# Inverse roots of queries and keys spread from the upper 64 rows of the array, directly behind the state value row's product in the lower 64

## Chip, cores and metric

The kernel runs on one core of one Trainium2 chip. The metric is the device time of one execution in microseconds (us); the median of three runs is given. TensorE multiplies and writes to the eight PSUM banks, VectorE and ScalarE move and change data, GpSimd (POOL) works on SBUF alone, SyncE (SP) issues DMAs.

## What is computed

One inference step of a decoder layer, for 256 prompt tokens and 8 sample tokens (one new token in each of 8 sequences), so 264 columns in all. A half feed-forward block, then a mixer with two branches that share one input projection, then a second half feed-forward block. The parts that matter here:

```python
qa, ka, va, qr, kr, vr, gr, ga, gb = split(h @ w_in)
# branch A: attention, 3 groups x 8 heads x 64, queries and keys normed per head
qa = rope(rmsnorm(qa, a_q_norm)) * A_SCALE
ka = rope(rmsnorm(ka, a_k_norm))
# branch B: retention, 4 heads, q and k of 256, v of 512; for each of the 8 sequences
state = state * gamma[h] + outer(k, v)      # 256 x 512, read, changed and written back
o = q @ state
```

The root mean square of queries and keys is over 64 features of a head. The retention state is 8 sequences x 4 heads, 32 matrices of 256 x 512.

## The kernel before

The activations stand transposed: features on the partitions, 264 tokens in the free dimension. A weight is streamed from HBM in halves of 128 x 1024 (512 KB). ScalarE rounds each half to fp32r (`wh`), VectorE takes the rest (`wl`, L428), and TensorE makes three passes for each 128 x 128 tile: `wh` with the high part of the activations, `wh` with their low part, `wl` with the high part (`three_passes`, L448 to L450). A half that makes one output tile is eight steps (k = 0 to 7) of three passes, `pe_wide_half`. Other small work of TensorE is put between the steps through the list `between`.

The order of work is written out by hand, half by half. After the projections of retention q, k and v come 16 halves of the gate (`gr`), then 24 halves for queries and keys (`qk`), 12 for the values (`v`), 8 for gate B (`gb`), 16 for projection B (`pb`), and so on. From the first query half on, the halves are numbered as slots: slots 0 to 11 are queries, 12 to 23 keys, 24 to 35 values. `slot_steps` says what TensorE does between the steps of slot s, and `qk_slot` what VectorE does in it.

State update. For each of the 32 states (sequence b, head h) TensorE broadcasts the value row of the sample to all partitions: `pe_state_v` multiplies a selector column, `pick`, repeated 128 times, with `vr_hl`, which has the high part of the eight value rows in partitions 0 to 7 and the low part in partitions 32 to 39, zeros elsewhere. The result is 128 x 512 in bank 6. VectorE then adds it, times k, to the state (`dve_state`, L1078), and TensorE multiplies the state with q in four narrow column groups (`pe_state_o`, L1087). States 0 to 7 are done in the gate's halves, at step 0 (for the first head once at step 5), states 8 to 31 in slots 1 to 32 (`STATE_SLOT`), each at step 0; at step 6 of every second slot stand the products with q and the sums of squares (`pe_qk_ms`, L927). Each state value product waits until VectorE has done the update before.

Norm of queries and keys. When the 12 query tiles have been squared and summed, ScalarE takes the root, VectorE its inverse, and ScalarE puts the 24 rows of 256 inverse roots (two heads in each of 12 tiles) in `qk_rinv`; `qk_rhl` has their high part in partitions 0 to 31 and their low part in 32 to 63 (`act_qk_rhi`, `dve_qk_rlo`). `pe_qk_spread` multiplies them with `sel` (128 x 128 for each tile), so that each row of a tile gets the inverse root of its head: two products of 256 columns for a pair of tiles, u, in the two halves of bank 4. VectorE multiplies the pair of tiles with it (`dve_qk_norm`, L1010). The next spread waits for that norm (`qk_done`). `SPREAD_AT` gives the slot of each spread: 18 to 23 for the queries, 28 to 33 for the keys, at step 4. In each slot VectorE's order is: shuffle for the rotation, the norm of this slot's spread, copy of a value tile, the update for the next slot's state value product, low part of the weights for four halves ahead.

After the last norm, `sp.wait_ge(qk_done, AT)` (L1545) lets SP load the first keys of the caches (L1236), with which VectorE starts in the first half of `gb` (`dve_key_product`, L1292). Ahead of this wait SP has issued the store of the last state and two large copies of the caches (`roll_more`, L1485).

A product that works on 64 partitions only is there once in the kernel before: `pe_scores` (L1146) multiplies queries and keys of 64 features, for two heads at a time, one on the lower and one on the upper 64 rows. Transposes and the products a_dec by v_ret (L829) work on fp32 as it is, all others named here on fp32r.

Of the kernel before, what the change touches and what calls it, by code (L numbers as in the profile page):

```python
# [7 lines left out]
F32 = mybir.dt.float32  # L8
F32R = mybir.dt.float32r
ALU = mybir.AluOpType  # L10
ACT = mybir.ActivationFunctionType
AX = mybir.AxisListType

P = 128
D = 1024
KD = D // P
S = 256
# [7 lines left out]
AH, AE = 8, 64  # L25
AW = AH * AE
AT = G * AW // P
RH, RQ, RV = 4, 256, 512
# [68 lines left out]
def build_tables():  # L97

    tab = np.zeros((P, NTAB), np.float32)

    def put(name, value):
        a, b = TABLES[name]
        value = np.asarray(value, np.float32)
        tab[:value.shape[0], a:b] = value.reshape(value.shape[0], b - a)

    pos = np.concatenate([np.arange(S), np.full(B, PAST)]).astype(np.float32)
    half = AE // 8
    inv = (np.float32(500000.0) ** (-np.arange(half, dtype=np.float32) / np.float32(half))).astype(np.float32)
    ang = (pos[None, :] * inv[:, None]).astype(np.float32).astype(np.float64)
    cos_a, sin_a = np.ones((P, T)), np.zeros((P, T))  # L110
    for base in (0, AE):
        for r in range(2):
            cos_a[base + r * half:base + (r + 1) * half] = np.cos(ang)
            sin_a[base + r * half:base + (r + 1) * half] = (-1.0 if r == 0 else 1.0) * np.sin(ang)
    put("cos_a", cos_a)
    put("sin_a", sin_a)
    head = np.zeros((P, HEADW))
    head[:AE, 2 * (AT - 1)] = 1.0
    head[AE:, 2 * (AT - 1) + 1] = 1.0
    put("head", head)  # L120
    put("sel", np.concatenate([np.eye(32), np.eye(32), np.zeros((64, 32))])[:, 0:2 * AT])
    put("seq", np.broadcast_to(np.eye(B).reshape(1, B * B), (P, B * B)))
    inv_r = (np.float32(1.0) / np.float32(10000.0) ** np.linspace(0.0, 1.0, P, dtype=np.float32)).astype(np.float32)
    ang_r = (pos[None, :] * inv_r[:, None]).astype(np.float32).astype(np.float64)
    put("cos_r", np.cos(ang_r))
    put("sin_r", np.sin(ang_r))
    token = 2 * (np.arange(S) % P) + np.arange(S) // P

    def allowed(g, queries, keys):
        dil = GROUPS[g][1]  # L130
        dist = token[queries][:, None] - token[keys][None, :]
        return np.where((dist >= 0) & (dist % dil == 0) & (dist // dil <= P), 0.0, NEG)

    first, second, both = slice(0, P), slice(P, S), slice(0, S)
    put("mask", np.concatenate([allowed(0, first, both), allowed(1, first, first), allowed(2, first, first),
                                allowed(0, second, both)], axis=1))
    gamma = 1.0 - 2.0 ** (-5.0 - np.arange(RH))
    decay = np.zeros((P, RH, 2, P))
    j, i = np.arange(P)[:, None], np.arange(P)[None, :]
    for h in range(RH):  # L140
        decay[:, h, 0] = np.where(i >= j, gamma[h] ** np.maximum(i - j, 0), 0.0)
        decay[:, h, 1] = gamma[h] ** (P + i - j)
    put("decay", decay)
    put("ident", np.eye(P))
    put("ones", np.ones((P, P)))
    put("blocks", np.kron(np.eye(2), np.ones((AE, AE))))
    kdec = np.zeros((P, RH, 2))
    for h in range(RH):
        for c in range(2):
            kdec[:, h, c] = gamma[h] ** (S - 1 - c * P - np.arange(P))  # L150
    put("kdec", kdec)
    put("gamma", np.broadcast_to(gamma, (P, RH)))
    row = np.arange(P)
    seq_at, head_at = row // 32, np.where(row % 32 < G * AH, row % 32, -1)
    put("rsel", (32 * (head_at // AH) + 28 + seq_at)[:, None] * np.where(head_at < 0, 0, 1)[:, None] == np.arange(100)[None, :])
    put("own_pick", (head_at[:, None] >= 0) & (head_at[:, None] % AH == np.arange(32)[None, :] // 4)
        & (seq_at[:, None] == np.arange(32)[None, :] % 4))
    put("own_head", np.arange(AH)[None, :] == (row % 32)[:, None])
    put("own_seq", np.arange(B)[None, :] % 4 == row[:, None] // 32)
    put("pick", (np.arange(PICK)[:, None] % 32 == np.arange(B)[None, :]))  # L160
    put("eps", np.full((P, 1), EPS))
    return tab


def trunk_step(nc, xT, tables, gains, w16, w11, cache0, cache1, cache2, state_in,
# [3 lines left out]
    with ExitStack() as ctx:  # L169
# [27 lines left out]
        pick = fixed("pick", [B], F32R)  # L197
# [54 lines left out]
        qk_rinv = at("qk_rinv", 93504, [S])  # L252
        qk_rinv4 = at("qk_rinv4", 90368, [AE])
        qk_rhl = at("qk_rhl", 94528, [S], F32R)
# [4 lines left out]
        vr_hl = at("vr_hl", 16384, [RH * RV], F32R)  # L259
# [37 lines left out]
        sel = nc.alloc_sbuf_tensor_at("sel", [P, AT * P], F32R, offset=tab_at + 4 * TABLES["cos_r"][0])  # L297
# [7 lines left out]
        bank4, bank5, bank6, bank7 = aux45[:, 0], aux45[:, 1], aux67[:, 0], aux67[:, 1]  # L305

        def sem(name):
# [27 lines left out]
        cleared, pick_done = sem("cleared"), sem("pick_done")  # L335
        qk_sq_done, qk_sq_s, qk_ms_psum, qk_rms_done, qk_rinv_done = (
            sem("qk_sq_done"), sem("qk_sq_s"), sem("qk_ms_psum"), sem("qk_rms_done"), sem("qk_rinv_done"))
        qk_rows, qk_rhi, qk_rlo, qks_ms, qks_rms, qks_rinv, qks_done = (
            sem("qk_rows"), sem("qk_rhi"), sem("qk_rlo"), sem("qks_ms"), sem("qks_rms"), sem("qks_rinv"), sem("qks_done"))
# [4 lines left out]
        vr_hi, vr_lo, vb_psum, state_scaled, state_new = (  # L344
            sem("vr_hi"), sem("vr_lo"), sem("vb_psum"), sem("state_scaled"), sem("state_new"))
# [29 lines left out]
        for q in range(QUADS):  # L375
            for s in range(2):
                n = 2 * q + s
# [564 lines left out]
        def act_qk_rhi(act, which):  # L942
            act.wait_ge(qk_rinv_done, which + 1)
            if which:
                act.wait_ge(qk_spread, AT // 2 * which)
            for e in range(4):
                nc.scalar.activation(qk_rinv[0:32, e * AE:(e + 1) * AE], qk_rinv4[32 * e:32 * e + 32], ACT.Copy).then_inc(qk_rows, 1)
            act.wait_ge(qk_rows, 4 * which + 4)
            nc.scalar.activation(qk_rhl[0:32], qk_rinv[0:32], ACT.Copy).then_inc(qk_rhi, 1)

        def dve_qk_rlo(dve, which):
            dve.wait_ge(qk_rhi, which + 1)
            nc.vector.tensor_tensor(qk_rhl[32:64], qk_rinv[0:32], qk_rhl[0:32].bitcast(F32),
                                    ALU.subtract).then_inc(qk_rlo, 1)

        def pe_qk_samples(pe):
# [39 lines left out]
        def pe_qk_spread(pe, u):  # L996

            pe.wait_ge(qk_rlo, 2 * u // AT + 1)
            if u:
                pe.wait_ge(qk_done, u)  # L1000
            for n in range(2):
                i = (2 * u + n) % AT
                last = nc.tensor.matmul(bank4[:, n * S:(n + 1) * S], sel[:, i * P:(i + 1) * P], qk_rhl[:], start=True, stop=True)
            last.then_inc(qk_spread, 1)

        def dve_qk_norm(dve, u):
# [33 lines left out]
        def pe_state_v(pe, s):  # L1040

            b, h = divmod(s, RH)
            if s:
                pe.wait_ge(state_new, 2 * s)
            else:
                pe.wait_ge(pick_done, 1)
                pe.wait_ge(vr_lo, 1)
                pe.wait_ge(q_owned, 1)
            if s == 2:
                pe.wait_ge(vr_lo, 2)  # L1050
            nc.tensor.matmul(bank6[:, :], pick[:, b:b + 1].to_broadcast([P, P]), vr_hl[:, h * RV:(h + 1) * RV], start=True, stop=True).then_inc(vb_psum, 1)  # L1051

        def act_rows_hi(act, part):

# [370 lines left out]

        fi1, fo1, p_qr, p_kr, p_vr, p_gr, p_qk, p_v, p_gb, p_pb, p_ga, p_pa, p_wo, fi2, fo2 = phases

        SPREAD_AT = {18 + u: u for u in range(AT // 2)}
        SPREAD_AT.update({28 + u: AT // 2 + u for u in range(AT // 2)})
        PAIR_STEP = 6  # L1430
        STATE_TURN = {s: [slot for slot in (s - 2, s - 1) if slot in STATE_SLOT] for s in range(2, 3 * AT - 3, 2)}
        STATE_TURN[3 * AT - 3] = [3 * AT - 4]
# [562 lines left out]
        def _(pool):  # L1995
# [20 lines left out]
            pool.wait_ge(os_psum, 6)  # L2016
            for n in (4, 5):
                pool.wait_ge(state_stored[n], 32)
            nc.gpsimd.memset(qk_rhl[:].bitcast(F32), 0.0).then_inc(cleared, 1)
            for t in range(2 * AT):  # L2020
                pool_qk_rot(pool, p_qk, t)
            pool_pack(pool)
# [17 lines left out]
        def _(pe):  # L2040
# [38 lines left out]
            def slot_steps(s):  # L2079


                steps = {k: [] for k in range(KD)}
                if s in STATE_SLOT:
                    steps[0].append(lambda: pe_state_v(pe, STATE_SLOT[s]))
                if s == 2:
                    steps[PAIR_STEP].append(lambda: pe_state_o(pe, EARLY_STATES - 1))
                for slot in STATE_TURN.get(s, ()):
                    steps[PAIR_STEP].append(lambda slot=slot: pe_state_o(pe, STATE_SLOT[slot]))
                if s % 2 == 0 and 2 <= s <= 2 * AT:
                    steps[PAIR_STEP] += [lambda: pe_qk_ms(pe, s - 2), lambda: pe_qk_ms(pe, s - 1)]  # L2090
                if s == 2 * AT + 2:
                    steps[1].append(lambda: pe_qk_samples(pe))
                if s in SPREAD_AT:
                    steps[4].append(lambda: pe_qk_spread(pe, SPREAD_AT[s]))
                return steps

            def bank_waits():
# [26 lines left out]
            for t in range(AT):  # L2124
                steps = slot_steps(RH * p_qk.quads + t)
# [170 lines left out]
```

## Time and profile before

| | us |
|---|---|
| median of 3 runs (lowest, highest) | 890.43 (890.13, 890.57) |
| profiled execution | 890.51 |
| its span | 888.4 |
| TensorE busy (PE) | 882.4, 99% |
| weight loads (PEld) | 854.5, 96% |
| VectorE busy (DVE) | 623.7, 70% |
| ScalarE busy (ACT) | 484.6, 55% |
| GpSimd busy (POOL) | 218.5, 25% |
| share of the time for which DMA packets were under way | 9 tenths or more in most of the 40 slices |

The profile was taken in one execution. A row of the timeline has the start in us from the span's start, the duration, the engine, the line of the kernel, the operation, what it writes and reads, and its shape; "128*64" before a matmul's shape is rows by columns of the array. Instructions of the same line that follow each other are merged, with their count behind x. PE is a matmul, PEld the weight load that belongs to it. A matmul's duration is a latency; the next one usually starts long before it ends. Idle time before an instruction stands in brackets, with what ended it.

### The profile page before, as it was taken

The numbers are of one execution on the slowest core, as the hardware profiler recorded it, in microseconds if no ns is written. First come the engines' busy times: TensorE is split into PE (matmuls) and PEld (weight loads), VectorE is DVE, ScalarE is ACT, GpSimd is POOL, SyncE is SP. The second block draws the span as 40 slices with busy tenths as digits, with TensorE's granted clock in tenths as the row PEclk, the third lists the DMA queues.
The fourth block names the chain that finished last, engine by engine and source line by source line (L and its number), as shares of the span: only waits on it lengthen the run. The fifth ranks groups of instructions, "written<-read, shape, count | busy, mean of one in ns | idle before, by whom it ended". The sixth has DMA issues, their size and how long they took to land.

```text
span 888.4 us, 19101 instructions
## 1 busy us (share of the span) xinstructions
PE 882.4 (99%) x7772; PEld 854.5 (96%) x7772; DVE 623.7 (70%) x917; ACT 484.6 (55%) x746; POOL 218.5 (25%) x239
## 2 busy tenths in 40 slices
PE   9999999999999999999999999999999999999998
PEld 8999999999999999999999999889899999999998
DVE  6666665568985588888887769985458666665543
ACT  6443444455544677677776556566646544443342
POOL 0433331004740000029875006000000043333000
PEclk9999999999999999999999999999999999999999
DMA  9998878999888778999997899787889899989771
GB/s 349 384 344 301 303 258 299 371 345 414 294 313 303 287 284 312 340 376 358 417 387 260 319 362 350 284 291 284 306 324 329 274 371 396 368 290 347 224 195 44
DMA packets 62054, 281.20 MB, mean 317 GB/s; under 512 B 7792, under 2 KB 8944, under 8 KB 60240
## 3 DMA queue, kind: packets, MB, share of 16 engines
q10 hardware_dynamic: 39024, 131.61, 43.6%
q1 hardware_dynamic: 22944, 148.37, 43.5%
q8 instruction: 62, 1.02, 0.5%
q14 instruction: 24, 0.20, 0.1%
HBM read 256.70 MB, written 111.32 MB: 414 GB/s over the span
## 4 chain that ended last, share of the span: by engine, by line
PE 90%; DVE 5%; DMA 2%; ACT 1%; issue 1%; ACTq 0%; POOL 0%; DVEq 0%
PE acc L448 16%; PE acc L449 15%; PE acc L450 15%; PE att L448 11%; PE att L449 10%; PE att L450 10%; DMA raw<-w 2%; PE aux L1087 2%; DVE wl L428 2%; PE att L1146 1%; PE att L1181 1%; PE att L1198 1%; PE aux L1051 1%; PE att L829 1%; PE att L746 1%
## 5 line engine op out<-in xcount | busy, mean ns | idle before, releaser
L428 DVE TENSOR_TENSOR wl<-raw,wh 128x1024 fp32r<-128x1024 f32 (+2 forms) x278 | 333.5, 1201 | 182.6 <-ACT wh L422 178.0
L422 ACT ACTIVATE wh<-raw 128x1024 fp32r<-128x1024 f32 (+2 forms) x278 | 275.2, 994 | 169.9 <-PE acc L450 89.6
L448 PE MATMUL acc<-hh,wh 128*128 128x264 f32 x496 | 145.4, 293 | 0.1
L449 PE MATMUL acc<-hl,wh 128*128 128x264 f32 x496 | 140.7, 284 | 0.0
L450 PE MATMUL acc<-hh,wl 128*128 128x264 f32 x496 | 140.6, 283 | 0.0
L448 PE MATMUL acc<-xh,wh 128*128 128x264 f32 x416 | 119.0, 286 | 0.4 <-DVE xl L556 0.4
L448 PE MATMUL att<-xh,wh 128*128 128x264 f32 x416 | 118.6, 285 | 0.4 <-DVE xl L556 0.3
L449 PE MATMUL att<-xl,wh 128*128 128x264 f32 x416 | 117.9, 283 | 0.0
L449 PE MATMUL acc<-xl,wh 128*128 128x264 f32 x416 | 117.8, 283 | 0.0
L450 PE MATMUL acc<-xh,wl 128*128 128x264 f32 x416 | 117.8, 283 | 0.0
L450 PE MATMUL att<-xh,wl 128*128 128x264 f32 x416 | 117.8, 283 | 0.0
L448 PEld LDWEIGHTS acc<-hh,wh 128*128 128x128 f32 x496 | 93.4, 188 | 2.3 <-issue 0.9
L449 PEld LDWEIGHTS acc<-hl,wh 128*128 128x128 f32 x496 | 93.5, 188 | 1.3
L450 PEld LDWEIGHTS acc<-hh,wl 128*128 128x128 f32 x496 | 93.2, 188 | 0.0
L448 PEld LDWEIGHTS acc<-xh,wh 128*128 128x128 f32 x416 | 78.3, 188 | 1.5 <-DVE xl L556 0.8
L630 POOL CAST uh<-product 128x264 fp32r<-128x264 f32 x44 | 31.0, 705 | 198.0 <-DVE product L619 198.0
L448 PEld LDWEIGHTS att<-xh,wh 128*128 128x128 f32 x416 | 78.3, 188 | 0.9 <-DVE xl L556 0.5
L449 PEld LDWEIGHTS att<-xl,wh 128*128 128x128 f32 x416 | 78.4, 188 | 0.1
L449 PEld LDWEIGHTS acc<-xl,wh 128*128 128x128 f32 x416 | 78.4, 188 | 0.0
L450 PEld LDWEIGHTS att<-xh,wl 128*128 128x128 f32 x416 | 78.0, 187 | 0.0
L450 PEld LDWEIGHTS acc<-xh,wl 128*128 128x128 f32 x416 | 78.0, 187 | 0.0
L598 ACT ACTIVATE silu<-square 128x264 f32<-128x264 f32 x44 | 18.7, 425 | 100.1 <-DVE square L612 100.1
(276 smaller groups left out, 2067.9 us busy)
## 6 DMA issues: line engine op xcount, KB each, us to landing
raw<-w ACTq DMA_DIRECT2D x207, 512.0 KB, 7.0
state<-state_in SPq DMA_DIRECT2D x32, 512.0 KB, 9.7
state_out<-state SPq DMA_DIRECT2D x32, 512.0 KB, 6.9
raw<-w ACTq DMA_DIRECT2D x32, 384.0 KB, 5.6
kv<-cache SPq DMA_DIRECT2D x24, 512.0 KB, 6.1
raw<-w ACTq DMA_DIRECT2D x32, 320.0 KB, 5.3
raw<-w SPq DMA_DIRECT2D x9, 512.0 KB, 9.5
kv_out<-cache SPq DMA_DIRECT2D x3, 960.0 KB, 7.2
```

The lines of the kernel that those rows point to most:

```text
L422: nc.scalar.activation(wh[n % HI_RING][:, 0:slot_size(n)], raw[n % RAW_RING][:, 0:slot_size(n)], ACT.Copy).then_inc(hi_done, 1)
L428: nc.vector.tensor_tensor(wl[n % RAW_RING][:, 0:slot_size(n)], raw[n % RAW_RING][:, 0:slot_size(n)], wh[n % HI_RING][:, 0:slot_size(n)].bi ...
L448: nc.tensor.matmul(out, w_hi, xh, start=first, stop=False)
L449: nc.tensor.matmul(out, w_hi, xl, start=False, stop=False)
L450: return nc.tensor.matmul(out, w_lo, xh, start=False, stop=last)
L598: nc.scalar.activation(silu[:, j // 2], gated[:, j // 2], ACT.Silu).then_inc(silu_done, 1)
L630: nc.gpsimd.tensor_copy(u_h, product[:, s]).then_inc(u_hi, 1)
L746: nc.tensor.transpose(rows[:, c * P:(c + 1) * P], part, ident)
L829: nc.tensor.matmul(out, v_ret[:, 0, cols], a_dec[:, 0:S], start=True, stop=False)
L1051: nc.tensor.matmul(bank6[:, :], pick[:, b:b + 1].to_broadcast([P, P]), vr_hl[:, h * RV:(h + 1) * RV], start=True, stop=True).then_inc(vb_p ...
L1087: last = nc.tensor.matmul(bank7[32 * e:32 * e + B, h * P:(h + 1) * P], q_own[:, 2 * h + p, b], state_of(s)[:, p * RV + e * P:p * RV + (e + ...
L1146: last = nc.tensor.matmul(out, qk[rows, t, qb:S:2], keys[:, qb] if n else keys, start=True, stop=True)
```

## The change

The spread's operands move to partitions 64 to 127: `sel` has its two unit blocks there, `qk_rinv` and `qk_rhl` are written at partitions 64 to 95 and 96 to 127. Both products are cut to 64 partitions: the state value product takes partitions 0 to 63 of `pick` and `vr_hl`, the spread partitions 64 to 127 of `sel` and `qk_rhl`. The spread goes from step 4 to step 0, right behind the slot's state value product where there is one. `SPREAD_AT` is set anew: 18, 19, 21, 22, 23, 25 for the queries and 29 to 34 for the keys; all but 31, 33 and 34 are slots with a state value product. The memset that cleared `qk_rhl` on GpSimd is gone, as no partition outside the cleared half is read.

```diff
-    put("sel", np.concatenate([np.eye(32), np.eye(32), np.zeros((64, 32))])[:, 0:2 * AT])
+    put("sel", np.concatenate([np.zeros((64, 32)), np.eye(32), np.eye(32)])[:, 0:2 * AT])
...
-                nc.scalar.activation(qk_rinv[0:32, e * AE:(e + 1) * AE], qk_rinv4[32 * e:32 * e + 32], ACT.Copy).then_inc(qk_rows, 1)
+                nc.scalar.activation(qk_rinv[64:96, e * AE:(e + 1) * AE], qk_rinv4[32 * e:32 * e + 32], ACT.Copy).then_inc(qk_rows, 1)
             act.wait_ge(qk_rows, 4 * which + 4)
-            nc.scalar.activation(qk_rhl[0:32], qk_rinv[0:32], ACT.Copy).then_inc(qk_rhi, 1)
+            nc.scalar.activation(qk_rhl[64:96], qk_rinv[64:96], ACT.Copy).then_inc(qk_rhi, 1)
...
-            nc.vector.tensor_tensor(qk_rhl[32:64], qk_rinv[0:32], qk_rhl[0:32].bitcast(F32),
+            nc.vector.tensor_tensor(qk_rhl[96:P], qk_rinv[64:96], qk_rhl[64:96].bitcast(F32),
                                     ALU.subtract).then_inc(qk_rlo, 1)
...
-                last = nc.tensor.matmul(bank4[:, n * S:(n + 1) * S], sel[:, i * P:(i + 1) * P], qk_rhl[:], start=True, stop=True)
+                last = nc.tensor.matmul(bank4[:, n * S:(n + 1) * S], sel[64:P, i * P:(i + 1) * P], qk_rhl[64:P], start=True,
+                                        stop=True)
...
-            nc.tensor.matmul(bank6[:, :], pick[:, b:b + 1].to_broadcast([P, P]), vr_hl[:, h * RV:(h + 1) * RV], start=True, stop=True).then_inc(vb_psum, 1)
+            nc.tensor.matmul(bank6[:, :], pick[0:64, b:b + 1].to_broadcast([64, P]), vr_hl[0:64, h * RV:(h + 1) * RV],
+                             start=True, stop=True).then_inc(vb_psum, 1)
...
-        SPREAD_AT = {18 + u: u for u in range(AT // 2)}
-        SPREAD_AT.update({28 + u: AT // 2 + u for u in range(AT // 2)})
+        SPREAD_AT = {18: 0, 19: 1, 21: 2, 22: 3, 23: 4, 25: 5, 29: 6, 30: 7, 31: 8, 32: 9, 33: 10, 34: 11}
...
-            nc.gpsimd.memset(qk_rhl[:].bitcast(F32), 0.0).then_inc(cleared, 1)
...
                 if s in STATE_SLOT:
                     steps[0].append(lambda: pe_state_v(pe, STATE_SLOT[s]))
+                if s in SPREAD_AT:
+                    steps[0].append(lambda: pe_qk_spread(pe, SPREAD_AT[s]))
...
-                if s in SPREAD_AT:
-                    steps[4].append(lambda: pe_qk_spread(pe, SPREAD_AT[s]))
```

## Rows read from the trace of the kernel before

**Rows 1.** Windows: stretch, busy us of each engine, clock, DMA share, GB/s.
```profile
240.00:515.00 275.00, 274.78 (x2661) 261.30 (x2660) 215.27 (x291) 179.99 (x282) 89.90 (x115) 1.00 0.90 329
537.00:564.00 27.00, 27.00 (x227) 26.68 (x226) 26.72 (x44) 15.79 (x21) 11.52 (x7) 1.00 0.99 375
```
**Rows 2.** Timeline of TensorE around one state value product.
```profile
435.38 0.28 PE L450 MATMUL att<-hh,wl 128*128 128x264 f32 x1
...
435.38 0.19 PEld L1051 LDWEIGHTS aux<-vr_hl,pick 128*128 128x128 f32 x1
...
435.50 0.39 PE L1051 MATMUL aux<-vr_hl,pick 128*128 128x512 f32 x1
...
435.73 0.28 PE L448 MATMUL acc<-hh,wh 128*128 128x264 f32 x1
```
**Rows 3.** Timeline of TensorE around one pair of spread products.
```profile
451.88 0.40 PE L1003 MATMUL att<-qk_rhl,sel 128*128 128x256 f32 x2
452.12 0.28 PE L448 MATMUL acc<-hh,wh 128*128 128x264 f32 x1
```
**Rows 4.** Timeline of TensorE around the first attention scores, in narrow windows.
```profile
562.34 0.28 PE L450 MATMUL acc<-obh,wl 128*128 128x264 f32 x1
562.55 0.51 PE L1146 MATMUL att<-qk 64*128 64x256 f32 x2
...
563.35 0.40 PE L1146 MATMUL att<-qk 64*128 64x128 f32 x4
...
563.46 0.28 PE L1146 MATMUL att<-qk 64*128 64x128 f32 x2
563.67 0.39 PE L448 MATMUL acc<-obh,wh 128*128 128x264 f32 x1
563.90 0.28 PE L449 MATMUL acc<-obl,wh 128*128 128x264 f32 x1
```
**Rows 5.** Groups of matmuls by shape: busy us, mean ns, idle before.
```profile
L829 PE MATMUL att<-a_dec,v_ret 128*128 128x256 f32 x32 | 9.6, 380 | 0.0
L1146 PE MATMUL att<-qk 64*128 64x256 f32 x32 | 5.8, 441 | 0.0
```
**Rows 6.** Timeline of the weight loads before the first scores.
```profile
562.54 0.20 PEld L1146 LDWEIGHTS att<-qk 64*128 64x128 f32 x2
```
**Rows 7.** Timeline of TensorE behind a group of narrow products.
```profile
438.78 0.39 PE L448 MATMUL acc<-hh,wh 128*128 128x264 f32 x1
439.01 0.29 PE L449 MATMUL acc<-hl,wh 128*128 128x264 f32 x1
```
**Rows 8.** Timeline of slots 21 and 22: state value products, update, norm.
```profile
462.50 0.39 PE L1051 MATMUL aux<-vr_hl,pick 128*128 128x512 f32 x1
...
463.00 1.41 DVE L1078 SCALAR_TENSOR_TENSOR state<-aux,kr_s,state 128x512 f32<-128x512 f32 x2 [1.52 <-PE aux L1051]
...
465.81 0.67 DVE L1010 TENSOR_TENSOR qk<-qk,att 128x512 f32<-128x512 f32 x1
...
465.87 0.39 PE L1051 MATMUL aux<-vr_hl,pick 128*128 128x512 f32 x1
```
**Rows 9.** Timeline at the change from slot 18 to slot 19.
```profile
454.10 0.66 DVE L1010 TENSOR_TENSOR qk<-qk,att 128x512 f32<-128x512 f32 x1
...
454.56 0.39 PE L1051 MATMUL aux<-vr_hl,pick 128*128 128x512 f32 x1
```
**Rows 10.** The cache copies before the keys: durations of issue, first and last start, landing.
```profile
L1485 SPq DMA_DIRECT2D kv_out<-cache x2: 665/790/915, 507.3 to 508.0; - x2
...
DMA to landing us min/median/max: 8.2/9.3/10.4
```
**Rows 11.** Timeline of SP's key loads and of VectorE until it uses them.
```profile
512.66 1.50 SPq L1236 DMA_DIRECT2D kv<-cache  x3
...
516.20 0.42 DVE L732 COPY v_tok<-att 128x256 f32<-128x256 f32 x1
...
525.48 1.22 DVE L1292 TENSOR_TENSOR kv<-kv,att 128x1024 f32<-128x1024 f32 x1 [0.56 <-DMA kv<-cache]
```

## The prediction

> **What bounds the kernel now.** I read the windows view first. Over the stretch of the retention gate and the attention projections, 240 to 515 us, TensorE is busy 274.78 of 275.00 us at a granted clock of 1.00, VectorE 215.27 us [rows 1]. But busy time is a sum of overlapping latencies here: a 128x264 pass is drawn with 0.28 us, while the next matmul starts 0.12 us after it [rows 2]. So the cost of a matmul is the distance from its start to the next start, and that is what I read everywhere below. As TensorE has no idle time to speak of, what is added between two starts is added to the end, and what is taken out is gained, unless another engine's work then comes late.
>
> The state value product (one per sequence and head, 32 in all) costs 0.23 us: it starts at 435.50 and the next pass at 435.73. Its weight load started at 435.38, under the pass ahead of it, so nothing is exposed [rows 2]. A pair of spread products costs 0.24 us (451.88 to 452.12) [rows 3]. Twelve such pairs are 2.9 us, which is the most that the change could hide.
>
> **What the change removes.** Nine of the twelve spreads (slots 18, 19, 21, 22, 23, 25, 29, 30, 32) now stand directly behind a state value product; slots 31, 33 and 34 have no state. The two products work on different halves of the array and write different banks. That such products run side by side is seen in the attention scores, which already work on 64 rows: two of 256 columns are both finished 0.51 us after the first one started [rows 4], where a single one takes 0.50 us (twice the mean of 441 ns less 380, see below) [rows 5]. So a pair that has the state product beside it costs about nothing: 9 x 0.24 = 2.15 us gained. The removed memset on POOL and the renamed partitions of the small copies cost or give nothing: POOL's memset has nobody waiting for its count, and the copies have the same number of columns.
>
> **What it adds: two changes of the array's shape around every state product.** This is the term that decides. Until now the state product contracts over all 128 partitions, as the passes on either side do. Afterwards it contracts over 64, and so do the spreads. The scores show what going to 64 rows and back costs [rows 4 to 6]:
> - going in, the first score starts 0.21 us after the last full pass (562.34 to 562.55), not 0.12: +0.09. Its weight load begins only at 562.54, beside it and not under the pass ahead [rows 6].
> - so the first product waits for its own weights: of the 32 score products of 256 columns, half are the first of a group. Their mean is 441 ns, where the same shape on full rows takes 380 [rows 5]. If the others take 380 too, the first ones take 502, so +0.12.
> - coming back, the last scores start at 563.46, the first full pass at 563.67: 0.21 us, where the products before had 0.11 (563.35 to 563.46): +0.10.
> - the first full pass has its load exposed: 563.67 to 563.90 is 0.23, not 0.12: +0.11 [rows 4].
>
> That is 0.42 us for one trip by rounded rows; I take 0.41. The narrow products on 8 and 32 columns pay the same way back: behind them a full pass is drawn with 0.39 us and the next starts 0.23 after it [rows 7]. So it isn't a peculiarity of the scores.
>
> There are 32 state products, none of which stands next to a group that changes the shape already: the narrow groups are at step 6 of a half, the state product at step 0 (in the first head at step 5). The three lone spreads make one trip each. 35 x 0.41 = +14.35 us. No state product of the gate phase gets anything in return, since no spread runs there, and 24 minus 9 in the slots get nothing either. Bounds: without the exposed load on the way in (the state product's load is 128 wide as the scores' was, so I don't expect that) a trip is 0.30 and the sum 10.5; the whole scores group, 1.56 us from 562.34 to 563.90, less two passes of 0.12, four pairs of 128 columns at 0.11 and two of 256 at twice that, leaves 0.44 for its trip [rows 4], and 35 x 0.45 is 15.75.
>
> The Trainium skill, "TensorEngine Tiling (Array Packing)", section "Key Properties", states that changing the tiling mode, and not just the tile, drains TensorE. That is a rule against this change, and the late loads and starts of the scores agree [rows 4, 6]. The same skill, "TensorE: Matmul & The Clock Gate", section "Measured speedup vs the span model", counts about 4 ns for each further tile of a pack; by that rule alone, with no drain, the sum would be the gain of 2.15 us and no more.
>
> **What it adds: a norm that must be finished earlier.** A spread waits until VectorE has consumed the one before from bank 4 (the norm, L1010). Behind the state product it stands four steps, twelve passes of 0.12 or 1.4 us, earlier in its slot than at step 4, and the main passes of TensorE stand behind it. The tight place is slot 22. VectorE's order in slot 21 is state update, low part of the weights, shuffle, norm: the state product of slot 21 starts at 462.50, the update at 463.00, the norm ends at 465.81 + 0.67 = 466.48, which is 3.98 us after the slot's start; slot 22 starts at 465.87, after 3.37 us [rows 8]. With the trip and without the spread at step 4 the slot becomes 3.37 + 0.41 - 0.24 = 3.54 us. The state product is ready 0.09 + 0.12 = 0.2 later, so the norm ends at 4.18, and a handover takes 0.1 (product finished at 462.89, update at 463.00). The spread would have started 0.09 into slot 22, so TensorE waits 4.18 + 0.1 - 3.54 - 0.09 = 0.65 us. In slot 19 the norm of slot 18 ends at 454.76, 0.2 us after the slot starts [rows 9]; VectorE is behind there and gains 0.4 us a slot on the longer TensorE, so I take 0.1. Elsewhere a slot without a spread lies between, or VectorE has more room. Sum +0.75 us, bounds 0 and 1.5.
>
> **What it moves: the last norm, one slot later.** SP loads the first keys of the cache only after norm 11. These loads start at 512.66, and VectorE's first product on them at 525.48, after 0.56 us of idle time [rows 11]. From there VectorE is full: 26.72 of 27.00 us from 537 to 564 [rows 1], and attention hangs on it. A late key would thus move the end nearly one for one. Norm 11 goes from slot 33 to slot 34, to where VectorE has the copy of 516.20 now [rows 11]; with 0.7 us for itself it ends at 516.9, 4.2 us later. What hides this: two cache copies were issued at 507.3 and 508.0 in the same queue and landed after 8.2 and 10.4 us, so until about 518.4 [rows 10]; I take it that the keys' packets come behind them. An issue at 516.9 rather than 512.66 still stands behind the copies, and TensorE itself is 3 x 0.41 longer over slots 32 to 34. I take +0.3 us; the cover gone, it is up to 4.
>
> **Sum.** +14.35 - 2.15 + 0.75 + 0.3 = +13.25 us. The profiled execution took 890.51 us, of which 888.4 is the span; the median of the runs shown is 890.43, so nothing has to be scaled: 890.43 + 13.2 = 903.6 us.
>
> **Rivals.**
> - No price for the shape. Place: the 35 trips. Products on 64 rows might slip in between full passes with their loads ahead, as the state product does today; the wait before the scores would then have been a wait for something else. The case turns where a trip costs less than (2.15 - 0.75)/35 = 0.04 us. Then it is 890.43 - 2.15 + 0.75 = 889.0. For it speaks that the products do run side by side [rows 4, 5]; against it, that the load of the scores starts 0.2 us behind the last pass and not with it [rows 4, 6], and that the narrow groups show the same on the way back [rows 7]. With the norm's wait at 0 too it would be 888.3, the only way to be faster by over 0.2%.
> - Half a price: one of the two ways is free, or the load in the middle is hidden. 35 x 0.2 = 7, so 890.43 + 7 - 2.15 + 1 = 896.3. The scores show all four parts separately [rows 4, 5], so this is less likely.
> - The change doesn't do what it says: the spread runs behind the state product and not beside it, because its two products share one half and have to load their own weights first. The 2.15 us are then not gained: 905.7.
> - The keys land late and VectorE's full stretch passes it on: 903.6 + 3.7 = 907.3.
>
> **How the numbers follow.** Forecast 0.73; spread not beside 0.07; keys late 0.08; half price 0.06; no price 0.06 (a third of that with the wait at nothing). Predicted is the likeliest, 903.6. The range takes in the trip's lower bound nearly (899.5) and late keys (907.5); outside are half price, no price and a little at the top. What the measurement can tell from no change is about 0.2%, or 1.8 us. So faster 0.02, same 0.04, slower 0.94.
>
> **What would show it.** The state product appears as 64*128 with 128x512 or 64x512 and about 0.50 us, 0.21 us behind the pass before it, and the first pass behind it with 0.39 us. The windows view of 240 to 430, with eight state products and no spread, must be longer by 8 x 0.41 = 3.3 us. The first spread product starts about 0.01 us behind the state product in seven of nine slots; in slot 22 TensorE's list of waits shows VectorE's L1010 with 0.4 to 0.8 us. If the state product keeps its 0.39 us and the passes around it 0.12, the forecast is wrong; if DMA kv appears among VectorE's waits with over 2 us, the third part was.

## The result

The changed kernel takes 902.61 us (median of four runs, 902.34 to 902.87), the kernel before 890.49 in the same comparison. The ratio is 1.0133, with a 95% interval from 1.0116 to 1.0150: 1.3% slower, 12.1 us. Predicted were 903.6 us and 13.25 us more. The profiled execution has a span of 900.2 us, 11.8 more than before, at a granted clock of 1.00.

### The profile page after: what moved, and what is told of

It reads as the page before. It is cut to its first block, busy times and chain, and to the rows that moved or that the text cites. A ratio compares the mean times of both kernels' runs of the same rounds, so it can differ in the third digit from the quotient of the medians.

```text
span 900.2 us, 19101 instructions
## 1 busy us (share of the span) xinstructions
PE 894.1 (99%) x7772; PEld 855.7 (95%) x7772; DVE 624.0 (69%) x917; ACT 485.1 (54%) x746; POOL 210.2 (23%) x238
## 4 chain that ended last, share of the span: by engine, by line
PE 90%; DVE 6%; issue 1%; ACT 1%; DMA 1%; ACTq 0%; SPq 0%; POOL 0%; DVEq 0%; POOLq 0%
PE acc L448 16%; PE acc L449 15%; PE acc L450 15%; PE att L448 11%; PE att L449 10%; PE att L450 10%; DVE wl L428 2%; PE aux L1089 2%; PE aux L1052 1%; DMA kv<-cache 1%; PE att L1148 1%; PE att L1183 1%; PE att L1200 1%; PE aux L2051 1%; PE att L829 1%
## 5 line engine op out<-in xcount | busy, mean ns | idle before, releaser
L448 PE MATMUL acc<-hh,wh 128*128 128x264 f32 x496 | 148.0, 298 | 0.1
```

What stands on the lines that cost most here:

```text
L448: nc.tensor.matmul(out, w_hi, xh, start=first, stop=False)
```

## The profile after

The windows view first, with the columns of [rows 1]. Nothing in it tells of the loss: TensorE is as full as before. (The second row covers other work than in [rows 1], since by then everything comes 11.5 us later.)

```profile
240.00:515.00 275.00, 274.47 (x2553) 251.97 (x2552) 208.97 (x282) 175.87 (x274) 81.16 (x114) 1.00 0.87 317
537.00:564.00 27.00, 27.00 (x312) 26.75 (x311) 26.07 (x30) 19.16 (x28) 13.90 (x9) 1.00 0.97 364
```

What does tell is the count behind PE: 2553 matmuls touch the same 275 us where there were 2661 before [rows 1]. TensorE does less in the same time and isn't idle by this view, since the longer starts hide under the latencies of 0.28 us and more.

The timeline of TensorE around a state value product that stands alone answers [rows 2]:

```profile
390.32 0.28 PE L450 MATMUL att<-hh,wl 128*128 128x264 f32 x1
390.54 0.49 PE L1052 MATMUL aux<-vr_hl,pick 64*128 64x512 f32 x1
390.96 0.39 PE L448 MATMUL att<-hh,wh 128*128 128x264 f32 x1
391.18 0.29 PE L449 MATMUL att<-hl,wh 128*128 128x264 f32 x1
```

The product starts 0.22 us behind the pass ahead (0.12 before), the next pass 0.42 behind it (0.23 before), and this pass is drawn with 0.39 us, like the one behind the scores in [rows 4]; the pass behind it starts after 0.22 us (0.12 for an ordinary pass). That is 0.86 us from 390.32 to 391.18. Around a product with a spread beside it, in slot 18:

```profile
457.71 0.28 PE L450 MATMUL att<-hh,wl 128*128 128x264 f32 x1
457.92 0.49 PE L1052 MATMUL aux<-vr_hl,pick 64*128 64x512 f32 x1
457.92 0.50 PE L1003 MATMUL att<-qk_rhl,sel 64*128 64x256 f32 x2
458.35 0.39 PE L448 MATMUL acc<-hh,wh 128*128 128x264 f32 x1
458.58 0.28 PE L449 MATMUL acc<-hl,wh 128*128 128x264 f32 x1
```

Both products start at 457.92. The pair is finished when the state product is, and the next pass starts 0.43 us behind, 0.01 more than without a spread. So the change does what it says: the spread is hidden. It has to be set against [rows 3], where the pair cost 0.24. From 457.71 to 458.58 are 0.87 us; without a change of shape it would be the 0.12 + 0.23 + 0.12 = 0.47 us of [rows 2] and, at step 4, another 0.24 for the spread. Hiding 0.24 us has cost 0.40.

The groups by shape show that every state product is like this, the 23 without a spread too (mean 493 ns; on 128 rows it is 394, as the kernel of an experiment below shows):

```profile
L1052 PE MATMUL aux<-vr_hl,pick 64*128 64x512 f32 x32 | 15.8, 493 | 0.0
L1003 PE MATMUL att<-qk_rhl,sel 64*128 64x256 f32 x24 | 5.9, 327 | 0.2 <-DVE qk L1011 0.2
```

Slot 22, where the norm was expected to be late, answers [rows 8]. First TensorE's timeline, then VectorE's:

```profile
473.62 0.28 PE L450 MATMUL att<-hh,wl 128*128 128x264 f32 x1
...
474.53 0.47 PE L1003 MATMUL att<-qk_rhl,sel 64*128 64x256 f32 x2 [0.20 <-DVE qk L1011]
474.93 0.39 PE L448 MATMUL acc<-hh,wh 128*128 128x264 f32 x1
```

```profile
473.71 0.67 DVE L1011 TENSOR_TENSOR qk<-qk,att 128x512 f32<-128x512 f32 x1
```

The norm ends at 473.71 + 0.67 = 474.38 and the spread starts at 474.53. From the pass at 473.62 to the pass at 474.93 are 1.31 us, where slot 18 has 0.64: a wait of 0.67 us. The bracket says 0.20, because only the part that isn't under the state product's latency counts as idle. A reader who took the list of waits for the price would be short by two thirds.

The keys answer [rows 10 and 11]. SP's timeline with the copies and the key loads, the landing of the two copies, and VectorE's first product on the keys:

```profile
517.79 1.40 SPq L1486 DMA_DIRECT2D kv_out<-cache  x2
527.76 4.82 SPq L1238 DMA_DIRECT2D kv<-cache  x6
```

```profile
DMA to landing us min/median/max: 8.2/9.1/9.9
```

```profile
536.94 1.22 DVE L1294 TENSOR_TENSOR kv<-kv,att 128x1024 f32<-128x1024 f32 x1 [0.53 <-DMA kv<-cache]
```

The load comes 15.1 us later than before (512.66), the product on it 11.5 us (525.48), which is TensorE's own delay; the idle time before it is 0.53 us where it was 0.56.

The first scores start at 574.07, where they started at 562.55 [rows 4]: 11.5 of the 11.8 us are lost before them, that is, in the stretch with the changed products.

```profile
574.07 0.51 PE L1148 MATMUL att<-qk 64*128 64x256 f32 x2
```

The other 0.3 us stand behind them, in one place. The second group of products of probabilities and cached values starts 0.55 us behind the last full pass (592.56), where it is 0.21 in the kernel before, and waits for its load:

```profile
593.11 1.06 PE L1390 MATMUL aux<-kv,dec_pT 128*32 128x512 f32 x8 [0.26 <-DMA kv<-cache]
```

This isn't shown to come from the change: two kernels below differ from the kernel before in the rows of the state product alone, and in their traces the same product starts still later behind its pass, 1.29 us (64 rows) and 0.97 us (96 rows).

## The experiments

The theory: each time that TensorE goes from full passes to products on 64 rows and back costs 0.39 us, whatever is done meanwhile, and the rest is small. Rivals: the price is of the spread's new place or of the pair; of having fewer rows than the neighbours; of the later keys. In all comparisons below, the kernel before ran on the same chip beside the others.

### One product of the two

The state value product on 64 rows, nothing else:

```diff
-            nc.tensor.matmul(bank6[:, :], pick[:, b:b + 1].to_broadcast([P, P]), vr_hl[:, h * RV:(h + 1) * RV], ...)
+            nc.tensor.matmul(bank6[:, :], pick[0:64, b:b + 1].to_broadcast([64, P]), vr_hl[0:64, h * RV:(h + 1) * RV], ...)
```

> The kernel before, with the state value product cut to partitions 0 to 63 and nothing else; the spreads stay on 128 rows at step 4. Theory (every product on 64 rows makes a trip of 0.39 us, as read in the changed kernel): 32 x 0.39 = +12.5 us, so 903.0 us, each state product drawn with 0.49 us, 0.21 behind the pass ahead. Rival (the price comes from the spread's new place, its wait or the pair of products, not from the rows): 890.5 us and 0.39 us for the product.

Measured 902.22 us against 890.67, ratio 1.0135 (1.0121 to 1.0149). Its product has the same 493 ns as in the changed kernel. The 11.55 us are 0.36 for each of 32 products; why this is not the 0.39 of the timeline is answered at the gate stage below. So this line alone makes the kernel as slow as the whole change does, without any spread moved.

The spread on the upper 64 rows, at its old place, and the state product as before (against the kernel before; the tables and copies that put its operands on partitions 64 to 127, as in the change, are left out here):

```diff
-                last = nc.tensor.matmul(bank4[:, n * S:(n + 1) * S], sel[:, i * P:(i + 1) * P], qk_rhl[:], start=True, stop=True)
+                last = nc.tensor.matmul(bank4[:, n * S:(n + 1) * S], sel[64:P, i * P:(i + 1) * P], qk_rhl[64:P], start=True,
+                                        stop=True)
```

> The changed kernel's spread on the upper 64 rows, but at step 4 in the old slots (18 to 23, 28 to 33), and the state value product on 128 rows as before. Theory: 12 trips of 0.39 = +4.7 us, 895.2 us. Rival (the upper half or the spread is free, all the price is of the state product): 890.5 us.

Measured 894.95 us, ratio 1.0051 (1.0037 to 1.0065): 4.3 us for 12 trips, 0.36 each. One of them in the timeline of TensorE:

```profile
492.28 0.28 PE L450 MATMUL att<-hh,wl 128*128 128x264 f32 x1
492.49 0.50 PE L1003 MATMUL att<-qk_rhl,sel 64*128 64x256 f32 x2
492.92 0.39 PE L448 MATMUL att<-hh,wh 128*128 128x264 f32 x1
493.14 0.28 PE L449 MATMUL att<-hl,wh 128*128 128x264 f32 x1
```

0.86 us from pass to pass, as for a state product alone. The two spread products of 256 columns take as long as the one of 512. The upper half isn't cheaper than the lower.

### Fewer rows, or another shape

```diff
-            nc.tensor.matmul(bank6[:, :], pick[:, b:b + 1].to_broadcast([P, P]), vr_hl[:, h * RV:(h + 1) * RV], ...)
+            nc.tensor.matmul(bank6[:, :], pick[0:96, b:b + 1].to_broadcast([96, P]), vr_hl[0:96, h * RV:(h + 1) * RV], ...)
```

> The kernel before, with the state value product cut to partitions 0 to 95 and nothing else. Theory (what costs is the change of the array's shape, which only 64 rows or fewer, or narrow columns, bring): 890.5 us, product 0.39 us with 0.12 before it. Rival (fewer rows than the neighbours cost by themselves): 903 us, as with 64.

Measured 890.73 us, ratio 1.0003 (0.9993 to 1.0012). The groups by shape of the state value product, on 64 rows (the kernel two above) and on 96:

```profile
L1051 PE MATMUL aux<-vr_hl,pick 64*128 64x512 f32 x32 | 15.8, 493 | 0.0
```

```profile
L1051 PE MATMUL aux<-vr_hl,pick 96*128 96x512 f32 x32 | 12.7, 398 | 0.0
```

With 96 rows the product is free of the price, with 64 it isn't. So having fewer rows than the neighbours doesn't cost by itself. That 64 rows fit a half of the array, which is then used in another shape, is the reading that fits both; the trace doesn't show the shape that the array is in, and no number between 64 and 96 was tried. This is the run that separates the theory from "a product unlike its neighbours is slow".

### The new places without the new shape

The changed kernel's `SPREAD_AT` and step 0, both products on 128 rows:

```diff
-        SPREAD_AT = {18 + u: u for u in range(AT // 2)}
-        SPREAD_AT.update({28 + u: AT // 2 + u for u in range(AT // 2)})
+        SPREAD_AT = {18: 0, 19: 1, 21: 2, 22: 3, 23: 4, 25: 5, 29: 6, 30: 7, 31: 8, 32: 9, 33: 10, 34: 11}
...
+                if s in SPREAD_AT:
+                    steps[0].append(lambda: pe_qk_spread(pe, SPREAD_AT[s]))
...
-                if s in SPREAD_AT:
-                    steps[4].append(lambda: pe_qk_spread(pe, SPREAD_AT[s]))
```

> The changed kernel's places (spread at step 0 behind the state product, slots 18, 19, 21, 22, 23, 25, 29 to 34), but both products on 128 rows and all partitions as before. Theory: no trip and nothing side by side, so only the waits for the norm (slots shorter by 0.24 us, so 0.3 us in slot 19 and 0.7 in slot 22) and up to 0.5 for the later keys: 891.5 us, between 890.5 and 892. Rival (the new places are what costs): about 902.

Measured 891.49 us, ratio 1.0006 (0.9993 to 1.0018), so not to be told from the kernel before by the times. The wait is where it was expected:

```profile
465.68 0.39 PE L1051 MATMUL aux<-vr_hl,pick 128*128 128x512 f32 x1
466.65 0.48 PE L1003 MATMUL att<-qk_rhl,sel 128*128 128x256 f32 x2 [0.58 <-DVE qk L1010]
466.97 0.28 PE L448 MATMUL acc<-hh,wh 128*128 128x264 f32 x1
```

The spread starts 0.97 us behind the state product, which takes 0.23, so 0.74 us are lost in slot 22. By the medians the places cost 0.8 us of the 12, and the interval allows 1.6 at most.

### Only where there is something beside

64 rows only in the nine slots with a spread beside the state product; the 23 others and the three lone spreads on 128 rows, and `qk_rhl` cleared again:

```diff
-            nc.tensor.matmul(bank6[:, :], pick[0:64, b:b + 1].to_broadcast([64, P]), vr_hl[0:64, h * RV:(h + 1) * RV],
+            rows = slice(0, 64) if any(STATE_SLOT.get(n) == s for n in SPREAD_AT) else slice(0, P)
+            nc.tensor.matmul(bank6[:, :], pick[rows, b:b + 1].to_broadcast([rows.stop, P]), vr_hl[rows, h * RV:(h + 1) * RV],
...
-                last = nc.tensor.matmul(bank4[:, n * S:(n + 1) * S], sel[64:P, i * P:(i + 1) * P], qk_rhl[64:P], start=True,
+                rows = slice(64, P) if any(SPREAD_AT.get(n) == u for n in STATE_SLOT) else slice(0, P)
+                last = nc.tensor.matmul(bank4[:, n * S:(n + 1) * S], sel[rows, i * P:(i + 1) * P], qk_rhl[rows], start=True,
```

> The changed kernel, but 64 rows only in the nine slots where a spread stands beside the state product; the other 23 state products and the three lone spreads work on 128 rows (the cleared halves are cleared again). Theory: 9 trips of 0.39 = +3.5, side by side -2.0, wait in slot 22 +0.65: 892.7 us. Below 890.5 would mean that a pair side by side is worth more than its trip.

Measured 892.59 us, ratio 1.0017 (1.0001 to 1.0034). In this kernel both shapes of the state product stand in one trace:

```profile
L1054 PE MATMUL aux<-vr_hl,pick 128*128 128x512 f32 x23 | 9.1, 394 | 0.0
...
L1054 PE MATMUL aux<-vr_hl,pick 64*128 64x512 f32 x9 | 4.4, 492 | 0.0
```

This is the best of the kernels tried with a pair, and it is still not faster than the kernel before: a trip of 0.39 us for 0.24 us hidden. Without the wait in slot 22 the nine pairs would by the same sizes still lose 9 x 0.39 - 2.0 = 1.5 us.

### The pair taken apart

The changed kernel, with its spreads at step 4 of the same slots, so never beside the state product:

```diff
-                if s in SPREAD_AT:
-                    steps[0].append(lambda: pe_qk_spread(pe, SPREAD_AT[s]))
...
+                if s in SPREAD_AT:
+                    steps[4].append(lambda: pe_qk_spread(pe, SPREAD_AT[s]))
```

> The changed kernel with the spreads at step 4 again, in the same slots and on the upper 64 rows, so never beside the state product. Theory: nine more trips and nothing side by side, 9 x (0.39 + 0.235 - 0.013) = +5.5, and no wait in slot 22, -0.66: 902.6 + 4.85 = 907.5 us. Rival (the pair brought nothing in the changed kernel, its two products run behind the state product): 902.6 + 3.5 - 0.7 = 905.4 us.

Measured 907.10 us, ratio 1.0168 (1.0139 to 1.0196), against 902.61 of the changed kernel in its own comparison. The rival's 905.4 would need the pair to have brought nothing; the time is nearer to 907.5, but the interval (1.0139 to 1.0196) takes in both. The traces decide it. The first scores start at 579.32 here and at 574.07 in the changed kernel, 5.25 us later (5.0 counted from the first product a_dec by v_ret), where the theory has 4.85 and the rival 2.8; and in the changed kernel's timeline the pair starts with the state product.

### The keys

The changed kernel with the last six spreads in slots 28 to 33:

```diff
-        SPREAD_AT = {18: 0, 19: 1, 21: 2, 22: 3, 23: 4, 25: 5, 29: 6, 30: 7, 31: 8, 32: 9, 33: 10, 34: 11}
+        SPREAD_AT = {18: 0, 19: 1, 21: 2, 22: 3, 23: 4, 25: 5, 28: 6, 29: 7, 30: 8, 31: 9, 32: 10, 33: 11}
```

> The changed kernel with the last six spreads one slot earlier (28 to 33 instead of 29 to 34), as many lone ones as before, so the first keys are asked for one slot earlier. Theory (the cache copies hide the later request): same as the changed kernel within 0.3 us, 902.6 us, and the keys' loads land no earlier against TensorE's work. Rival (the later request costs): 0.5 us or more faster than the changed kernel.

Measured 902.30 us, ratio 1.0113 (1.0084 to 1.0142). It was not on the chip beside the changed kernel, so 0.3 us between them mean nothing. It also has a wait of its own: the first key spread, in slot 28, comes before VectorE has its low part, and starts 0.54 us behind its pass (498.21) and not 0.21. A gain of that size from earlier keys would be hidden in the time.

```profile
498.75 0.47 PE L1003 MATMUL att<-qk_rhl,sel 64*128 64x256 f32 x2 [0.26 <-DVE qk_rhl L953]
```

The trace of the keys themselves is clearer:

```profile
518.65 1.53 SPq L1486 DMA_DIRECT2D kv_out<-cache  x2
523.98 5.68 SPq L1238 DMA_DIRECT2D kv<-cache  x6
```

```profile
536.84 1.22 DVE L1294 TENSOR_TENSOR kv<-kv,att 128x1024 f32<-128x1024 f32 x1 [0.20 <-DMA kv<-cache]
```

The keys are asked for at 523.98 rather than 527.76, 3.8 us earlier, and the first product on them starts at 536.84 rather than 536.94. Both products waited for their load, so the earlier request brought its landing forward by 0.1 us only. In both kernels the copies ahead of it in the queue were issued at about 518 and take up to 10 us. That the keys' packets wait behind those is the likely reason, which no run here singled out.

### The other direction: fewer changes of shape

If a change of shape costs, the kernel before can be made faster by having fewer. In the gate stage each head has two groups of narrow columns (q times state) in different halves. Three of the eight were moved to stand directly ahead of another:

```diff
-                                                      6: ([lambda: pe_state_o(pe, 2 * h - 1)] if h else []) + [lambda: ret_a(h)]})
+                                                      6: ([lambda: pe_state_o(pe, 2 * h - 2), lambda: pe_state_o(pe, 2 * h - 1)] if h else []) + [lambda: ret_a(h)]})
...
-                                                      6: [lambda: pe_state_o(pe, 2 * h), lambda: pe_ret_sum(pe, h)]})
+                                                      6: ([lambda: pe_state_o(pe, 2 * h)] if h == RH - 1 else []) + [lambda: pe_ret_sum(pe, h)]})
```

> The kernel before, with the product of q and state 2h (narrow columns) moved from step 6 of the fourth half of head h to the place of the next one, state 2h + 1, in the first half of head h + 1, for the first three heads: three groups of narrow columns fewer. Theory (each group pays for its change of shape, 0.3 us without a wide load on the way in): 3 x 0.3 = 0.9 us faster, 889.6 us. Rival (the places of the narrow groups cost nothing, or the states' buffers come free too late): 890.5 us or more.

Measured 889.84 us against 890.77, ratio 0.9980 (0.9966 to 0.9994). It ran once more, beside the kernel of the next experiment:

> The kernel with merged narrow groups once more, on the same chip as the one with both, so that the two can be compared: 889.8 us.

889.99 us against 891.45, ratio 0.9985 (0.9976 to 0.9994). The gate stage, from the first product a_dec by v_ret to the first sum of squares, in the timelines of the kernel before, the merged one and its second run:

```profile
306.89 0.60 PE L829 MATMUL att<-a_dec,v_ret 128*128 128x256 f32 x2
...
394.36 0.41 PE L927 MATMUL att<-qk_sq,tab 128*32 128x64 f32 x16
```

```profile
306.28 0.59 PE L829 MATMUL att<-a_dec,v_ret 128*128 128x256 f32 x2
...
392.80 0.41 PE L927 MATMUL att<-qk_sq,tab 128*32 128x64 f32 x16
```

```profile
306.70 0.59 PE L829 MATMUL att<-a_dec,v_ret 128*128 128x256 f32 x2
...
393.26 0.41 PE L927 MATMUL att<-qk_sq,tab 128*32 128x64 f32 x16
```

87.47 us, 86.52 and 86.56: 0.9 us less for three groups, twice. In the traces of the four other kernels of this document whose gate stage is that of the kernel before (spread on 64 rows, 96 rows, full rows, only beside), it takes 87.49 to 87.52, so 0.9 us is far more than these traces differ by themselves. This version is the fastest here: 0.15 to 0.2% under the kernel before by the ratios, 0.9 and 1.5 us by the medians.

The same was tried in the attention stage, on top of the merged kernel: the narrow products of probabilities and cached values go between the transposes and the scores.

```diff
+                late = u > ATT_AT and not second
                 for n in DEC_V.get(u, ()):
-                    dec.append(lambda n=n: pe_dec_v(pe, n))
+                    if not late:
+                        dec.append(lambda n=n: pe_dec_v(pe, n))
...
                         steps[2].append(lambda: pe_turn(pe, i - 1, 1))
+                    for n in DEC_V.get(u, ()):
+                        steps[2].append(lambda n=n: pe_dec_v(pe, n))
```

> The kernel with merged narrow groups, and in the attention stage three of the products of probabilities and cached values (32 columns) moved behind the transposes of their step, so that they stand directly ahead of the scores: one change of shape fewer at each (narrow to 64 rows, rather than narrow to full and full to 64 rows). Theory: 3 x 0.2 = 0.6 us more than the merged kernel gains, 889.3 us where the kernel before has 890.6. Rival (those products are late for the gather, or the change from narrow to 64 rows costs as much as two): no faster than the merged kernel, 889.8 us.

Measured 890.82 us against 891.45, ratio 1.000 (0.999 to 1.001). The theory's 889.3 was missed and what the merged kernel gained is gone by the ratio; the medians still leave 0.6 us of it. Four of the twelve executions took 892.8 to 893.5 us.

The group was moved in three places. In the first, TensorE's timeline of the merged kernel (its second run) and of this one:

```profile
570.13 0.28 PE L450 MATMUL acc<-obh,wl 128*128 128x264 f32 x1
570.86 1.06 PE L1388 MATMUL aux<-kv,dec_pT 128*32 128x512 f32 x8 [0.45 <-ACT dec_own L1378]
...
573.57 0.39 PE L448 MATMUL acc<-obh,wh 128*128 128x264 f32 x1
```

```profile
570.30 0.28 PE L450 MATMUL acc<-obh,wl 128*128 128x264 f32 x1
570.79 0.66 PE L1181 MATMUL att<-tab,prob 128*128 128x128 f32 x4 [0.21 <-ACT prob L1174]
...
573.50 0.39 PE L448 MATMUL acc<-obh,wh 128*128 128x264 f32 x1
```

The transposes (L1181), now in front, wait for ScalarE's probabilities. But on its old place the narrow group waited longer, for ScalarE's `dec_own`, and from the last pass to the next it is 3.20 us now and was 3.44: 0.24 less. In the third place it is 2.77 us (633.45 to 636.22) and was 2.92 (632.85 to 635.77), 0.15 less and without a wait in either. The second place loses more than that:

```profile
582.35 1.06 PE L1388 MATMUL aux<-kv,dec_pT 128*32 128x512 f32 x8 [0.74 <-DMA kv<-cache]
...
584.48 0.39 PE L448 MATMUL acc<-obh,wh 128*128 128x264 f32 x1
```

From the pass at 580.89 to the one at 584.48 are 3.59 us, where the merged kernel has 2.92 (580.97 to 583.88): the group waits for the load of its cached values, although it is asked for later in its step than before. The kernels with the state product alone on 64 and on 96 rows have the same wait on the group's old place, and the changed kernel a shorter one, so the wait isn't shown to come from the move. In this trace the change of shape that is saved is thus there, 0.15 us in the place without waits rather than the 0.2 expected, and a late load hides it. Only one execution was profiled: whether this load is what keeps the median 0.8 us above that of the merged kernel stays open.

## Why the prediction was right

By its own steps:

- What bounds the kernel. Right: TensorE's starts add up to the span. Over the stretch with all changed products the delay of the first scores (11.5 us) is nearly that of the end (11.8).
- The trip. Forecast 0.41 us, bounds 0.30 and 0.45. A lone state product: 0.22 and not 0.12 before it (+0.10), 0.42 and not 0.23 to the next pass (+0.19), its successor 0.22 and not 0.12 (+0.10), together 0.39. The whole says the same: 0.86 us from 390.32 to 391.18, as for the lone spread of 492.28 to 493.14, against 0.47. The forecast's middle two parts, +0.12 and +0.10, came out as 0.19 together. The +0.12 had been taken from the latency of the first scores; the distance to the next start is what counts, as the prediction itself had said, and it is a bit smaller. 35 x 0.02 = 0.7 us of the miss.
- The gate stage, which has state products and no spread. Foretold were 3.3 us more for eight products, to be seen in the window of 240 to 430 us. That sign could not be read: a window of fixed times doesn't get longer, and this one holds 17 state products of the kernel before. From the first product a_dec by v_ret to the first sum of squares, a stretch with ten state products, the changed kernel takes 91.05 us, where the kernel before takes 87.47 (its rows stand with the merged kernel above): 3.6 us.

```profile
306.69 0.38 PE L829 MATMUL att<-a_dec,v_ret 128*128 128x256 f32 x1
...
397.74 0.41 PE L927 MATMUL att<-qk_sq,tab 128*32 128x64 f32 x16
```

  Ten trips of 0.39 would be 3.9. The missing 0.3 us are three products v_lo by k_hi (L882), which start 0.33 us behind their predecessor in the kernel before and 0.23 in the changed one; the first of them, before and after:

```profile
334.87 0.49 PE L881 MATMUL att<-v_hi,k_hi 128*128 128x512 f32 x1
335.19 0.39 PE L882 MATMUL att<-v_lo,k_hi 128*128 128x512 f32 x1
```

```profile
335.84 0.39 PE L881 MATMUL att<-v_hi,k_hi 128*128 128x512 f32 x1
336.07 0.39 PE L882 MATMUL att<-v_lo,k_hi 128*128 128x512 f32 x1
```

  The three delays stand in every trace with the state product on full rows or on 96 in this stage, and in none of the four with 64. What TensorE waited for there isn't shown, as no list of waits has it; it was covered by the longer TensorE. So a trip costs 0.39 us here too, and 0.36 is what it adds on average, since a little of it falls on waits.

- Side by side. Forecast -2.15; the pair adds 0.01 and not 0, so -2.0.
- The norm in slot 22. Forecast 0.65, measured 0.67. Slot 19, taken at 0.1, has 0.66 us from pass to pass (462.21 to 462.87) where slot 18 has 0.64, so 0.02. The sign named for slot 22, 0.4 to 0.8 us in TensorE's list of waits, failed all the same: the list has 0.20.
- The keys. Forecast +0.3, bounds 0 and 4. The first product on the keys moved with TensorE, and the idle time before it is 0.53 where it was 0.56, so 0. The cover held. The load that came 0.3 us late behind the scores was not in the forecast.
- The sum with the measured sizes: 35 x 0.39 - 2.0 + 0.67 + 0 = +12.3 us, against 12.1 measured. That the rest is only 0.2 is in part luck: the three waits in the gate stage that fell away (-0.3) and the late load behind the scores (+0.3) stand in no term and cancel.

The rivals: "no price for the shape" and "half a price" fell with the first timeline; "not beside" fell with the pair that starts together at 457.92; "keys late" with the idle time. The rule that the prediction drew from the Trainium skill, "TensorEngine Tiling (Array Packing)", section "Key Properties", that a change of mode drains the engine, agrees with the traces as far as they go: a lone product on 64 rows starts 0.22 us behind a full pass and the next full pass 0.42 behind it, where it was 0.12 and 0.23. They don't tell a drain from weights that are loaded too late. What was measured decided against the gain that concurrency by itself gives.

The one kernel whose time lay clearly beside its expectation is the last. In its trace two of the three places save time, 0.24 and 0.15 us, and the one between them loses 0.67 to a late load, for which the expectation had no term.

## What to carry to other kernels

Before packing small matmuls beside each other in parts of the array, count how often the array would leave its full shape and come back: here 0.39 us for each time, so that a pair must hide more than that, and every product that is cut down for the pair's sake pays even where it has no partner. Products of the same shape belong together: three groups fewer gave 0.9 us here. But a gain of a few tenths per place is as large as the waits that come and go between executions (0.3 to 1.1 us for one load here), so read it from pass to pass in the trace, place by place, and look at the old place too before a wait is put down to the move. And where a full engine is slower without being idle, compare distances between starts and counts in a window, since neither busy time nor the list of waits shows it.

## What the runs showed of the hardware

- A product over 96 partitions is as cheap as one over 128 (398 and 394 ns, and the median ratio 1.0003), one over 64 takes 493 ns and adds 0.39 us together with the late starts around it.
- A wait under a latency is shown at less than its size: 0.67 us lost in slot 22 and 0.20 in the list; 0.74 and 0.58 on full rows.
- Two products of 256 columns on one half, with weights of their own, take as long as one of 512, 0.50 us, where the pair takes 0.40 on full rows [rows 3]. The second is drawn with 0.28 us in both, so it starts about 0.22 us behind the first and not 0.12. Why isn't shown; beside a product of 512 it doesn't matter.
- In pairs on the two halves, both products start within 0.01 us in slot 18 (457.92).
